# The last pair of gate columns projected behind the values, with transposes and two short attention units inside its product

## The chip, the cores and the metric

The kernel runs on one core of one Trainium2 chip. The metric is the device time of one execution in microseconds (us), taken as the median of several runs. A core has five engines that each run their own stream in order and meet only at semaphores: TensorE (PE, matrix products), VectorE (DVE), ScalarE (ACT), GpSimd (POOL) and SyncE (SP, which here issues the DMA transfers).

## What is computed

One layer of a hybrid backbone over 256 context tokens and 1024 latent tokens, all float32. What matters here is the input projection, whose columns the kernel takes in 16 pairs of 128, and the attention that follows.

```python
h = rms_norm(x, lp['norm1_g']) * (1 + sc1) + sh1
proj = h @ lp['w_in']                       # 1024 -> 4096 columns
q, k, v, xp, ga, gb = jnp.split(proj, cuts, axis=-1)
q, k = per-head RMS norm, rotary on latent tokens
k_all = concat(cached k (512), k)           # latent queries only
attn = block_attention(q, k_all, v_all)     # context queries: 256 context keys alone
merged = sigmoid(ga) * (attn @ w_branch_a) + sigmoid(gb) * (pool @ w_branch_b)
```

## The kernel before

Every float32 operand of a product is split in a high and a low part of the type float32r, and a product is three matmuls: high by high, high by low, low by high. `project(n, j)` (matmul at L324) makes 128 columns (half j of pair n) for all 1280 tokens: eight chunks k of the 1024 inputs, nine matmuls each, into one of two PSUM halves. `hooks` is a table from a chunk number to other PE work that is issued behind that chunk. The weights of a pair are loaded by SP into `w_raw`; ACT rounds them to `w_hi` (L451), POOL subtracts to `w_lo` (L539). PE waits for `w_hi`, `w_lo` and `ps_free` (the PSUM half read out) before a product.

The first block of the kernel runs the pairs in this order: 2 of pooling input, 8 of gates, 4 of queries, the keys (K0), the values (V0). In the gate loop, hooks behind chunks 4 and 7 also multiply two blocks of the modulation weights (`ada_block`, `ada_turn`), whose rows DVE copies and adds (`loop_rows`, `loop_mods`). ACT applies the sigmoid to each gate half (L474) and SP stores it in DRAM (`gates`).

The keys of head j are normed by DVE (L715), rotated by DVE and POOL (L722, L557, L725), rounded by ACT into `kT_hi` (L518) and subtracted by POOL into `kT_lo` (L560). They lie in `kraw`, whose first buffer is the tile `stage`; the first values buffer `vraw[0]` is the same tile. ACT therefore copies the values out of PSUM (L525) only once both L560 are done (`k_lo`). PE then turns each half (ten transposes, L417) in groups n = 0 to 5, and ACT (L530, even n) and DVE (L744, odd n) copy them into `vals`. Last, ACT rounds the cached keys (L532) and POOL subtracts them (L562). All this stands behind the last product. Then a barrier of all engines, at which the semaphores are cleared (L750), ends the block.

The attention block has 16 latent units (four heads, 128 queries, 1536 keys) and 4 short ones (context queries, 256 keys). For a latent unit, a `head` is nine score matmuls (L875 to L877), the maximum on DVE (L1022 to L1025), and the exponential on ACT (L946); the scores of the next head wait for it, because they write the same PSUM banks. The opening of the block is written out: for g = 0 to 4 it issues `head(units[g // 4], g % 4)`, then for the short unit g its scores (L915 to L917), and for unit g-1 the turn (L926), the copies (L970 on ACT, L1051 on DVE) and the value product (L934). Only then come the transposes (L901) and value products (L885) of unit 0 between the further heads of unit 1. POOL splits the queries first (L987, L990; short ones L1000, L1002), after clearing `stage` (L1011) for the zero fill of `y_sum` (L862).

Of the kernel before, what the change touches and what calls it, by code (L numbers as in the profile page):

```python
# [71 lines left out]
def build(nc, io, last_block=99):  # L72
    with ExitStack() as ctx:
# [76 lines left out]
        vraw = [stage, at("vraw1", [P, TOK], F32, RHL)]  # L150
        kc_raw = at("kc_raw", [P, KV, PAST], F32, RHL + 8 * KB)

        s = {}
        for n in ("eps_r x_ss rs_used consts rope wpool_in icnt_in x_sq x_scaled xT_ps xT_outa xT_outd c_in c_sig c_silu fa_mm fa_rows fa_turn fa_mods ada_mm0 ada_mm1 ada_rows0 ada_rows1 ada_turn mods_r0 mods_r1 ada_in0 ada_in1 "
                  "mods_b h_raw h_hi_r h_lo_r w_in0 w_hi0 w_hi1 w_lo0 w_lo1 mm0 mm1 ps_free0 ps_free1 pad0 xp_in xp_used "
                  "d_done gate_r0 gate_r1 gate_st0 gate_st1 py_ps py_out py_st sq_r0 sq_r1 ss_mm rt_sq rt_r rs_mm rs_out q_raw q_sin q_cos q_fin "
                  "k_fin k_hi k_lo kout v_raw vout v_ps v_out_a v_out_d cache_in cache_hi cache_lo dve_c").split():
# [4 lines left out]
        XP_PAIRS, GATE_PAIRS, Q_PAIRS = 2, 8, 4  # L162
        G0, Q0, K0, V0 = 2, 10, 14, 15
# [7 lines left out]
        ROWS_AT = AUX[0]  # L171
        FIRST = (0, 4, 1, 5, 2, 6, 3, 7)
# [8 lines left out]
        with nc.Block() as block:  # L181
            @block.sync
            def _(sp):
# [18 lines left out]
                def load_ada(n, j):  # L202
                    if isinstance(n, int):
# [10 lines left out]
                for c in range(4):  # L214
# [3 lines left out]
                    if c == 1:  # L218
                        load_w(2)

                def store_gate(i, j):
                    sp.wait_ge(s[f"gate_r{j}"], i + 1)
                    sp.dma_start(io["gates"][bass.ds(2 * i + j, 1)].rearrange("o p n -> p (o n)"), gst[j][:]).then_inc(s[f"gate_st{j}"], 16)
                with sp.Fori(0, GATE_PAIRS - 1) as i:
                    load_w(i + G0 + 1)
                    load_ada(i + 5, 0)
                    store_gate(i, 0)
                    load_ada(i + 5, 1)
# [15 lines left out]
                for j in range(2):  # L244
                    sp.wait_ge(s["q_raw"], HEADS + j + 1)
                    sp.dma_start(io["out_k"][j], kraw[j][:, 0:CTX]).then_inc(s["kout"], 16)
                for j in range(2):
                    sp.wait_ge(s["v_raw"], j + 1)
                    if j == 1:
                        sp.dma_start(kc_raw[:], io["cache_k"]).then_inc(s["cache_in"], 16)  # L250
                        sp.wait_ge(s["k_fin"], 2)
                        sp.dma_start(vals[:, TILES:KEY_TILES, :], io["cache_v"]).then_inc(s["cache_in"], 16)
                    sp.dma_start(io["out_v"][j], vraw[j][:, 0:CTX]).then_inc(s["vout"], 16)
                sp.wait_ge(s["kout"], 32)
                sp.wait_ge(s["vout"], 32)
                for j in range(2):
                    sp.wait_ge(s[f"gate_st{j}"], 16 * GATE_PAIRS)
                sp.wait_ge(s["cache_in"], 32)

            @block.tensor  # L260
            def _(pe):
# [98 lines left out]
                for n in range(1, XP_PAIRS):  # L360
                    project(n, 0)
                    project(n, 1)
                with pe.Fori(0, GATE_PAIRS) as i:
                    for j in range(2):
                        project(i + G0, j, hooks={4: lambda: ada_block(i + 4, j), 7: lambda: ada_turn(i + 4, j)})
# [40 lines left out]
                project(V0, 1)  # L406

                for j in range(2):
                    pe.wait_ge(s["v_raw"], j + 1)
                    for q, (g, w) in enumerate(GROUPS):  # L410
# [1680 lines left out]
```

## Time and profile before

| | us |
|---|---|
| median of 3 runs | 1818.58 |
| lowest and highest run | 1817.08 and 1820.91 |
| the profiled execution | 1816.4 |
| its span, first to last instruction | 1814.5 |
| PE busy (share of the span) | 1616.6 (89%) |
| DVE, ACT, POOL busy | 898.6, 593.2, 393.8 |

The profiled execution is 1.9 us longer than its span, for what lies before the first and behind the last instruction. The median of the runs is 2.2 us above the profiled one. The views used below are the page, its windows (busy time by stretch with the granted TensorE clock, where 1.00 is 2.4 GHz and 0.50 is 1.2 GHz), and the timeline, where an entry in brackets gives the idle time before an instruction and what ended it.

### The profile page before, as it was taken

The page shows a single profiled execution, that of the slowest core. Times are in us where ns is not written, and L with a number is a line of the kernel's source. Part 1 is how long each engine was busy: PE and PEld are TensorE (multiplying, and loading weights), DVE is VectorE, ACT ScalarE, POOL GpSimd, SP SyncE. Part 2 cuts the span into 40 slices and gives each one's busy share as a digit, 9 for nine tenths or more (in the row PEclk, how much of TensorE's full clock was granted, in tenths as well). Part 3 has the DMA queues.
Part 4 walks back from the last instruction along what each step waited for, and adds up shares of the span by engine and source line. Part 5 has one row for each costly group of instructions (what it writes and reads, how often), then busy time and mean ns, then how long its engine had stood idle before and what let it go on. Part 6 is the DMA issues. An engine that isn't in the chain of part 4 may idle for free. (4 is left out here: it accounts for less than half of the span.)

```text
span 1814.5 us, 22464 instructions
## 1 busy us (share of the span) xinstructions
PE 1616.6 (89%) x8410; PEld 1278.2 (70%) x8410; DVE 898.6 (50%) x1257; ACT 593.2 (33%) x764; POOL 393.8 (22%) x252
## 2 busy tenths in 40 slices
PE   4899999999999699999999899989977399999950
PEld 4688888878887466666666588878866288888840
DVE  5560000006565666676666543341147667666638
ACT  5211121232222444444444500021123055555513
POOL 1011111112223400000000121121116234445420
PEclk8999999999999899999999999999998599999985
DMA  8133434230100500000000133213032179898945
GB/s 350 67 115 135 159 132 143 109 119 23 46 23 9 200 1 0 0 1 1 0 0 0 58 139 121 85 53 124 23 114 105 65 233 295 266 290 277 281 77 218
DMA packets 38016, 202.28 MB, mean 111 GB/s; under 512 B 4304, under 2 KB 5072, under 8 KB 27728
## 3 DMA queue, kind: packets, MB, share of 16 engines
q1 hardware_dynamic: 28752, 168.07, 24.0%
q0 software_dynamic: 9216, 33.56, 8.3%
q8 instruction: 31, 0.51, 0.1%
q14 instruction: 17, 0.14, 0.0%
HBM read 154.43 MB, written 47.19 MB: 111 GB/s over the span
## 5 line engine op out<-in xcount | busy, mean ns | idle before, releaser
L324 PE MATMUL psum<-h_hi,w_hi 128*128 128x512 f32 (+1 forms) x768 | 199.3, 368 | 7.3 <-DVE h_lo L624 5.5
L324 PE MATMUL psum<-h_lo,w_hi 128*128 128x512 f32 (+1 forms) x768 | 193.6, 361 | 0.0
L324 PE MATMUL psum<-h_hi,w_lo 128*128 128x512 f32 (+1 forms) x768 | 192.5, 359 | 0.0
L885 PE MATMUL psum<-probT,vals 128*128 128x512 f32 x384 | 190.9, 593 | 0.0
L946 ACT ACTIVATE prob<-psum,nmax 128x1536 f32<-128x1536 f32 x64 | 98.6, 1541 | 209.5 <-DVE nmax L1025 209.5
L324 PEld LDWEIGHTS psum<-h_hi,w_hi 128*128 128x128 f32 x768 | 128.7, 190 | 34.7 <-issue 14.3
L539 POOL TENSOR_TENSOR w_lo<-w_raw,w_hi 128x1024 fp32r<-128x1024 f32 x32 | 77.0, 2408 | 348.2 <-ACT w_hi L451 348.2
L901 PEld LDWEIGHTS psum<-ident,prob 128*128 128x128 f32 x768 | 93.0, 141 | 78.6 <-issue 72.7
L324 PEld LDWEIGHTS psum<-h_lo,w_hi 128*128 128x128 f32 x768 | 128.8, 190 | 23.1
L324 PEld LDWEIGHTS psum<-h_hi,w_lo 128*128 128x128 f32 x768 | 128.5, 189 | 23.1
L1022 DVE TENSOR_REDUCE rmax<-psum 128x1 f32<-128x512 f32 x192 | 128.9, 688 | 31.1 <-PE psum L877 30.8
L901 PE MATMUL psum<-ident,prob 128*128 128x128 f32 x768 | 110.7, 274 | 7.9 <-PE psum L885 7.9
L875 PE MATMUL psum<-kT_hi,q_hi 128*128 128x512 f32 x192 | 96.7, 504 | 10.1 <-POOL q_lo L990 8.7
L591 DVE COPY ada_rows<-psum 128x256 f32<-128x256 f32 x24 | 10.2, 425 | 159.7 <-PE psum L279 159.4
L853 DVE COPY probT<-psum 128x512 f32<-128x512 f32 x64 | 44.3, 691 | 85.3 <-PE psum L901 85.3
L1645 POOL DMA_INDIRECT y_sum<-yst,y_row x32 | 74.9, 2340 | 26.0 <-POOL y_row L1643 26.0
L877 PE MATMUL psum<-kT_hi,q_lo 128*128 128x512 f32 x192 | 76.1, 396 | 0.0
L853 ACT COPY probT<-psum 128x512 f32<-128x512 f32 x128 | 70.0, 586 | 18.0 <-PE psum L901 18.0
L876 PE MATMUL psum<-kT_lo,q_hi 128*128 128x512 f32 x192 | 75.3, 392 | 0.0
L885 PEld LDWEIGHTS psum<-probT,vals 128*128 128x128 f32 x384 | 61.6, 190 | 17.4 <-issue 16.1
L1817 DVE TENSOR_TENSOR gu_lo<-gu_raw,gu_hi 128x3072 fp32r<-128x3072 f32 x15 | 50.4, 3358 | 47.5 <-ACT gu_hi L1760 47.5
L987 POOL CAST q_hi<-qT 128x512 fp32r (+1 forms) x16 | 9.7, 609 | 295.4 <-PE psum L877 295.4
(326 smaller groups left out, 3026.3 us busy)
## 6 DMA issues: line engine op xcount, KB each, us to landing
gu_raw<-in_w_gu SPq DMA_DIRECT2D x16, 2048.0 KB, 9.4
ada<-in_w_ada SPq DMA_DIRECT2D x20, 1024.0 KB, 4.8
w_raw<-in_w_in SPq DMA_DIRECT2D x16, 1024.0 KB, 4.8
dn_raw<-in_w_dn SPq DMA_DIRECT2D x16, 1024.0 KB, 6.9
gates<-gst SPq DMA_DIRECT2D x16, 640.0 KB, 3.0
wm_raw<-in_w_merge SPq DMA_DIRECT2D x4, 1536.0 KB, 7.8
y_sum<-stage SPq DMA_DIRECT2D x12, 512.0 KB, 11.9
xt<-in_x SPq DMA_DIRECT2D x10, 512.0 KB, 8.0
```

The costliest lines, as they stand in the source:

```text
L324: mm = pe.matmul(psum[:, par_sets[j] + g:par_sets[j] + g + w], a[j][:, k, :], b[:, k, g:g + w], start=(k == 0 and a is w_hi and b is h_hi) ...
L539: nc.gpsimd.tensor_tensor(w_lo[j][:], w_raw[:, :, j * P:(j + 1) * P], w_hi[j][:], ALU.subtract).then_inc(s[f"w_lo{j}"], 1)
L853: copy(probT[b][g % 2][:], psum[:, TP + 512 * b:TP + 512 * b + 512]).then_inc(s[f"a_t_out{b}"], 1)
L875: pe.matmul(o, q_hi[x.par][:, g, :], kT_hi[:, x.kv, k], start=True, stop=False)
L876: pe.matmul(o, q_hi[x.par][:, g, :], kT_lo[:, x.kv, k], start=False, stop=False)
L877: pe.matmul(o, q_lo[x.par][:, g, :], kT_hi[:, x.kv, k], start=False, stop=True).then_inc(s["a_scored"], 1)
L885: mm = pe.matmul(psum[:, PV + 512 * x.par:PV + 512 * x.par + 512], vals[:, x.key0 // P + c, x.kv * HD:(x.kv + 1) * HD], probT[b][g % 2][:] ...
L901: mm = pe.transpose(psum[:, o:o + P], prob[x.par][:, h, c * P:(c + 1) * P], ident[:])
L946: nc.scalar.activation(prob[x.par][:, g, 0:x.keys], psum[:, SC:SC + x.keys], ACT.Exp, bias=nmax[:, x.par, g:g + 1], scale=SCALE, accum_out ...
L1022: ins = nc.vector.reduce_max(rmax[:, b:b + 1], psum[:, SC + 512 * b:SC + 512 * (b + 1)], AX.X)
L1645: nc.gpsimd.indirect_dma_start(io["y_sum"], bass.IndirectOffsetOnAxis(y_row[j][:], 0), yst[j][:], None, compute_op=ALU.add).then_inc(s[f"e ...
L1817: tt(gu_lo[q][:, 0:GU_FIRST, :], gu_raw[q][:, 0:GU_FIRST, :], gu_hi[q][:, 0:GU_FIRST, :], ALU.subtract).then_inc(s[f"e_gu_lo{q}"], 1)
```

## The change

The pair order of the projection becomes 2 pooling, 7 gates, 4 queries, keys, values, and then the eighth gate pair (L0). Modulation blocks 4 to 11 had been the hooks of the eight gate pairs; now the second pooling pair carries the hooks of block 4, the gate loop those of blocks 5 to 11, and L0 none. The value transposes (`turn_v`) become hooks: groups 0 to 2 behind chunks 4 to 6 of the second half of the values, groups 3 to 5 behind chunks 1 to 3 of L0's first half. The cached keys are loaded earlier to another place and split between the weight splits of L0. The short units 0 and 1 run as hooks of L0 (scores, turn, values), with their own tiles and semaphores; the attention block keeps units 2 and 3, and POOL has split unit 2's queries already. The clearing of `stage` moves behind the first short value step. The late sigmoids use the tile of the cached keys and `stage`, and SP stores them before the barrier.

```diff
-        XP_PAIRS, GATE_PAIRS, Q_PAIRS = 2, 8, 4
-        G0, Q0, K0, V0 = 2, 10, 14, 15
+        XP_PAIRS, GATE_PAIRS, Q_PAIRS = 2, 7, 4
+        G0, Q0, K0, V0, L0 = 2, 9, 13, 14, 15
...
+                    for j in range(2):
+                        project(n, j, hooks={4: lambda: ada_block(4, j), 7: lambda: ada_turn(4, j)})
...
-                project(V0, 1)
...
+                def turn_v(n):
+                    j, (g, w) = n // 3, GROUPS[n % 3]
                     pe.wait_ge(s["v_raw"], j + 1)
...
+                def early_score(z):
+                    pe.wait_ge(s["s_q"], 2 * z + 2)
+                    pe.wait_ge(s["k_lo"], 2)
...
+                    for g in range(GRP):
+                        o = psum[:, AUX[0] + CTX * g:AUX[0] + CTX * (g + 1)]
+                        pe.matmul(o, sq_hi[:, g, :], kT_hi[:, 0, 0:CTX], start=True, stop=False)
+                        pe.matmul(o, sq_hi[:, g, :], kT_lo[:, 0, 0:CTX], start=False, stop=False)
+                        mm = pe.matmul(o, sq_lo[:, g, :], kT_hi[:, 0, 0:CTX], start=False, stop=True)
+                    mm.then_inc(s["s_scored"], 1)
...
+                def early_turn(z):
+                    pe.wait_ge(s["s_normed"], z + 1)
+                    for c in range(2):
+                        for h in range(GRP):
...
+                def early_value(z):
+                    pe.wait_ge(s["gate_r0"], GATE_PAIRS + 1)
+                    pe.wait_ge(s["s_pv_out"], z)
...
+                project(V0, 1, hooks={4: lambda: turn_v(0), 5: lambda: turn_v(1), 6: lambda: turn_v(2)})
+                project(L0, 0, hooks={1: lambda: turn_v(3), 2: lambda: turn_v(4), 3: lambda: turn_v(5), 5: lambda: early_score(0)})
+                project(L0, 1, hooks={0: lambda: early_turn(0), 1: lambda: early_value(0), 2: lambda: early_score(1),
+                                      5: lambda: early_turn(1), 6: lambda: early_value(1)})
...
+                v_rows(0)
+                split(L0, 0)
+                act.wait_ge(s["ck_in"], 16)
                 nc.scalar.copy(kT_hi[:, :, TOK:KEYS], kc_raw[:]).then_inc(s["cache_hi"], 1)
+                v_out(0)
+                v_out(2)
+                v_rows(1)
+                split(L0, 1)
+                v_out(4)
+                early_exp(0)
+                act.wait_ge(s["cache_lo"], 1)
+                late_gate(0)
...
+                early_turned(0)
+                early_values(0)
+                early_exp(1)
+                early_turned(1)
+                early_values(1)
+                late_gate(1)
...
+                    if c in (1, 2):
+                        loop_rows(4, c - 1)
+                        loop_mods(4, c - 1)
...
-        short = [Unit(z, z // 2, z % 2 * P, 0, CTX, 0) for z in range(4)]
...
+        short = [Unit(z, z // 2, z % 2 * P, 0, CTX, 0) for z in range(SHORT_EARLY, 4)]
...
-    order = [6, 7] + list(range(8, 16)) + [0, 1, 2, 3] + [4, 5]
+    order = [6, 7] + list(range(8, 15)) + [0, 1, 2, 3] + [4, 5] + [15]
```

PE before, the end of the second half of the values (L324, the last chunk) and the transposes (L417). A semaphore in brackets is what the instruction waits for; `vraw_113` is the second values buffer.

```order
L324 MATMUL psum<-h_hi,w_lo_86 128x512 x2
L324 MATMUL psum<-h_hi,w_lo_86 128x256
L417 MATMUL psum<-ident,stage 128x128 [waits b1_rs_out,b1_v_raw]
L417 MATMUL psum<-ident,stage 128x128 x7
L417 MATMUL psum<-ident,stage 128x128 [waits b1_v_out_a]
L417 MATMUL psum<-ident,stage 128x128
L417 MATMUL psum<-ident,vraw_113 128x128 [waits b1_v_out_d,b1_v_raw]
L417 MATMUL psum<-ident,vraw_113 128x128 x3
L417 MATMUL psum<-ident,vraw_113 128x128 [waits b1_v_out_a]
L417 MATMUL psum<-ident,vraw_113 128x128 x3
L417 MATMUL psum<-ident,vraw_113 128x128 [waits b1_v_out_d]
L417 MATMUL psum<-ident,vraw_113 128x128
```

PE after, in the middle of the same half (its product is now L338, the transposes L429): the end of chunk 4, hook, chunk 5, and the next hook.

```order
L338 MATMUL psum<-h_hi,w_lo_86 128x256
L429 MATMUL psum<-ident,stage 128x128 [waits b1_rs_out,b1_v_raw]
L429 MATMUL psum<-ident,stage 128x128 x3
L338 MATMUL psum<-h_hi,w_hi_84 128x512 x2
L338 MATMUL psum<-h_hi,w_hi_84 128x256
L338 MATMUL psum<-h_lo,w_hi_84 128x512 x2
L338 MATMUL psum<-h_lo,w_hi_84 128x256
L338 MATMUL psum<-h_hi,w_lo_86 128x512 x2
L338 MATMUL psum<-h_hi,w_lo_86 128x256
L429 MATMUL psum<-ident,stage 128x128 [waits b1_v_raw]
L429 MATMUL psum<-ident,stage 128x128 x3
```

The first transpose with its wait for `v_raw` now has three chunks of the values' product queued behind it.

ACT before, from the second rounding of keys to the end of the first block:

```order
L518 CAST kT_hi<-kraw_112 128x1280 [waits b1_k_fin]
L525 COPY stage<-psum 128x1280 [waits b1_mm0,b1_kout,b1_k_lo]
L525 COPY vraw_113<-psum 128x1280 [waits b1_mm1]
L530 COPY vals<-psum 128x4x128 [waits b1_v_ps,b1_k_fin,b1_q_fin]
L530 COPY vals<-psum 128x2x128 [waits b1_v_ps]
L530 COPY vals<-psum 128x4x128 [waits b1_v_ps]
L532 CAST kT_hi<-kc_raw 128x2x512 [waits b1_cache_in]
```

ACT after, from the early exponentials of unit 0 (L588) to the end of the block; L582 is the late sigmoid, L594 and L598 copy the turned scores and the values of a short unit:

```order
L588 ACTIVATE sprob_early,short_sum<-psum,short_nmax 128x256 x3
L582 ACT_TABLE_LOAD [waits b1_mm0]
L582 ACTIVATE gst_late_115<-psum 128x1280 [waits b1_cache_lo]
L594 COPY sprobT_early_119<-psum 128x512 [waits b1_s_turned,b1_s_pv,b1_vout,b1_v_ps]
L598 COPY qT<-psum 128x4x128 [waits b1_s_pv]
L588 ACT_TABLE_LOAD [waits b1_s_turned]
L588 ACTIVATE sprob_early,short_sum<-psum,short_nmax 128x256 [waits b1_s_neg_max]
L588 ACTIVATE sprob_early,short_sum<-psum,short_nmax 128x256 x3
L594 COPY sprobT_early_119<-psum 128x512 [waits b1_s_pv,b1_s_turned]
L598 COPY qT<-psum 128x4x128 [waits b1_s_pv]
L582 ACT_TABLE_LOAD
L582 ACTIVATE stage<-psum 128x1280 [waits b1_mm1]
```

The last work of ACT in the block is now a sigmoid of the product that ends last, where it was the rounding of the cached keys. The load of the last sigmoid's function table stands ahead of the wait for `mm1`.

DVE before, the third and fourth steps of the attention opening (L1022 maximum of a head, L1040 maximum of a short unit, L1047 its norm, L1051 its copy):

```order
L1040 TENSOR_REDUCE short_max<-psum 128x4
L1041 TENSOR_SCALAR short_nmax<-short_max 128x4
L1034 RECIPROCAL einv<-esum 128x1
L1036 TENSOR_SCALAR prob_2663<-prob_2663,einv 128x1536
L1046 RECIPROCAL short_inv<-short_sum 128x4
L1047 TENSOR_TENSOR sprob<-sprob,short_inv 128x1024
L1022 TENSOR_REDUCE rmax<-psum 128x1 x3
L1024 TENSOR_REDUCE rmax<-rmax 128x1
L1025 TENSOR_SCALAR nmax<-rmax 128x1
L1051 COPY sprobT_2679<-psum 128x512
L1040 TENSOR_REDUCE short_max<-psum 128x4
```

DVE after, from the copy of the last short unit (L1171) on:

```order
L1171 COPY sprobT_3033<-psum 128x512
L1154 RECIPROCAL einv<-esum 128x1
L1156 TENSOR_SCALAR prob_3019<-prob_3019,einv 128x1536
L1142 TENSOR_REDUCE rmax<-psum 128x1 x3
L1144 TENSOR_REDUCE rmax<-rmax 128x1
L1145 TENSOR_SCALAR nmax<-rmax 128x1
L1154 RECIPROCAL einv<-esum 128x1
L1156 TENSOR_SCALAR prob_3019<-prob_3019,einv 128x1536
L1142 TENSOR_REDUCE rmax<-psum 128x1 x3
L1144 TENSOR_REDUCE rmax<-rmax 128x1
```

Between two maxima of a head stand only the norm of the head before, where there were also a copy, a maximum and a norm of a short unit.

## Rows read from the trace of the kernel before

**Rows 1.** The page: head, and DMA issues of the gates (last: us to landing).

```profile
span 1814.5 us, 22464 instructions
...
gates<-gst SPq DMA_DIRECT2D x16, 640.0 KB, 3.0
```

**Rows 2.** Windows: length, busy us per engine (instructions), granted clock, DMA share, GB/s.

```profile
585.00:602.00 17.00, 5.25 (x22) 3.71 (x20) 1.81 (x3) 6.22 (x7) 6.74 (x6) 0.58 0.33 110
...
602.00:645.00 43.00, 30.95 (x142) 22.00 (x143) 31.71 (x53) 19.21 (x49) 17.96 (x14) 0.94 0.45 171
```

**Rows 3.** Timeline: start us, us, engine, line, operation, count, [idle before].

```profile
570.77 0.54 PEld L324 LDWEIGHTS psum<-h_hi,w_hi 128*128 128x128 f32 x3
...
570.77 4.97 DVE L722 TENSOR_TENSOR rtmp<-kraw,sin 32x1024 f32<-32x1024 f32 x4 [0.34 <-DVE kraw L715]
...
579.69 0.75 PE L324 MATMUL psum<-h_hi,w_hi 128*128 128x512 f32 x3
...
583.72 2.91 POOL L560 TENSOR_TENSOR kT_lo<-kraw,kT_hi 128x1280 fp32r<-128x1280 f32 x1 [2.52 <-ACT kT_hi L518]
...
584.38 0.74 PE L324 MATMUL psum<-h_hi,w_lo 128*128 128x512 f32 x3
...
586.66 1.23 ACT L525 COPY stage<-psum 128x1280 f32<-128x1280 f32 x1 [3.02 <-POOL kT_lo L560]
...
587.94 2.56 PE L417 MATMUL psum<-ident,stage 128*128 128x128 f32 x10 [2.81 <-ACT stage L525]
```

**Rows 4.** Timeline, from the last split of the first block to the first attention score.

```profile
595.34 2.34 POOL L562 TENSOR_TENSOR kT_lo<-kc_raw,kT_hi 128x1024 fp32r<-128x1024 f32 x1 [8.72 <-ACT kT_hi L532]
...
599.04 0.95 POOL L1011 MEMSET stage<- 128x1024 f32 x1 [1.36 <-POOLq L750]
...
602.04 0.80 PE L875 MATMUL psum<-kT_hi,q_hi 128*128 128x512 f32 x1 [8.70 <-POOL q_lo L990]
```

**Rows 5.** Timeline of PE, the beginning of the attention block.

```profile
608.52 0.50 PE L875 MATMUL psum<-kT_hi,q_hi 128*128 128x512 f32 x1 [1.41 <-ACT prob L946]
...
618.46 0.80 PE L875 MATMUL psum<-kT_hi,q_hi 128*128 128x512 f32 x1
...
625.12 1.96 PE L934 MATMUL psum<-sprobT,vals 128*128 128x512 f32 x4 [1.71 <-ACT sprobT L970]
...
641.94 3.26 PE L934 MATMUL psum<-sprobT,vals 128*128 128x512 f32 x4 [3.31 <-ACT sprobT L970]
...
646.65 0.48 PE L875 MATMUL psum<-kT_hi,q_hi 128*128 128x512 f32 x1
```

**Rows 6.** Timeline, second pooling pair: start of its product, end of the second pooled channel.

```profile
88.63 0.83 PE L324 MATMUL psum<-h_hi,w_hi 128*128 128x512 f32 x3 [0.51 <-issue]
...
100.39 1.69 DVE L694 TENSOR_TENSOR dpool<-dpool,xpad 128x256 f32<-128x256 f32 x2
```

**Rows 7.** Windows after two idle stretches of PE (columns as in rows 2).

```profile
587.90:594.20 6.30, 5.12 (x20) 3.71 (x20) 1.81 (x3) 2.65 (x4) 0.00 (x0) 0.50 0.61 208
...
602.00:604.80 2.80, 2.76 (x7) 2.20 (x8) 0.69 (x1) 0.00 (x0) 1.82 (x2) 0.50 1.03 281
```

**Rows 8.** Timeline of PE, one short unit: scores, turn, next scores, values.

```profile
605.53 0.27 PE L915 MATMUL psum<-kT_hi,sq_hi 128*128 128x256 f32 x1
...
606.84 0.28 PE L917 MATMUL psum<-kT_hi,sq_lo 128*128 128x256 f32 x1
...
612.66 1.10 PE L926 MATMUL psum<-ident,sprob 128*128 128x128 f32 x8 [1.77 <-DVE sprob L1047]
...
613.51 0.36 PE L915 MATMUL psum<-kT_hi,sq_hi 128*128 128x256 f32 x1
...
617.06 1.95 PE L934 MATMUL psum<-sprobT,vals 128*128 128x512 f32 x4 [1.89 <-ACT sprobT L970]
```

**Rows 9.** Timeline of ACT, first sigmoid of the gate loop.

```profile
132.42 1.28 ACT L474 ACT_TABLE_LOAD   x1 [13.06 <-PE psum L324]
...
133.71 1.24 ACT L474 ACTIVATE gst<-psum 128x1280 f32<-128x1280 f32 x1
```

More of the change, by code:

```diff
@@ L149, in build @@
         kraw = [stage, at("kraw1", [P, TOK], F32, RKV + 40 * KB)]
-        vraw = [stage, at("vraw1", [P, TOK], F32, RHL)]
-        kc_raw = at("kc_raw", [P, KV, PAST], F32, RHL + 8 * KB)
+        vraw = [stage, at("vraw1", [P, TOK], F32, RKV + 45 * KB)]
+        kc_raw = at("kc_raw", [P, KV, PAST], F32, RKV + 50 * KB)
+        gst_late = [at("gst_late0", [P, TOK], F32, RKV + 50 * KB), stage]
+        sq_hi = at("sq_hi", [P, GRP, P], F32R, RW)
+        sq_lo = at("sq_lo", [P, GRP, P], F32R, RW + 2 * KB)
+        sprob_early = at("sprob_early", [P, GRP, CTX], F32, RW + 4 * KB)
+        sprobT_early = [at(f"sprobT_early{c}", [P, GRP * P], F32, RKV + (45 + 2 * c) * KB) for c in range(2)]
         s = {}
@@ L360, in _ @@
                 for n in range(1, XP_PAIRS):
[L361 to L362 removed]
+                    for j in range(2):
+                        project(n, j, hooks={4: lambda: ada_block(4, j), 7: lambda: ada_turn(4, j)})
                 with pe.Fori(0, GATE_PAIRS) as i:
                     for j in range(2):
[L365 removed]
+                        project(i + G0, j, hooks={4: lambda: ada_block(i + 5, j), 7: lambda: ada_turn(i + 5, j)})
                 pe.wait_ge(s["wpool_in"], 16)
@@ L528, in _, with v_out, late_gate @@
-                for n in range(0, 6, 2):
+                    act.wait_ge(s["v_raw"], j + 1)
+                    act.sem_inc(s[f"ps_free{j}"], 1)
+                def v_out(n):
                     act.wait_ge(s["v_ps"], n + 1)
                     nc.scalar.copy(*v_chunk(n)).then_inc(s["v_out_a"], 1)
-                act.wait_ge(s["cache_in"], 32)
-                nc.scalar.copy(kT_hi[:, :, TOK:KEYS], kc_raw[:]).then_inc(s["cache_hi"], 1)
+                def late_gate(j):
+                    act.wait_ge(s[f"mm{j}"], L0 + 1)
+                    nc.scalar.activation(gst_late[j][:], psum[:, par_sets[j]:par_sets[j] + TOK], ACT.Sigmoid).then_inc(s[f"gate_r{j}"], 1)
@@ new lines, in early_exp, with early_turned @@
+                def early_exp(z):
+                    act.wait_ge(s["s_neg_max"], z + 1)
+                    act.wait_ge(s["s_turned"], 2 * z)
+                    for g in range(GRP):
+                        nc.scalar.activation(sprob_early[:, g, :], psum[:, AUX[0] + CTX * g:AUX[0] + CTX * (g + 1)], ACT.Exp,
+                                             bias=short_nmax[:, g:g + 1], scale=SCALE, accum_out=short_sum[:, g:g + 1]).then_inc(s["s_exped"], 1)
+                def early_turned(z):
+                    act.wait_ge(s["s_turned"], 2 * z + 1)
+                    act.wait_ge(s["s_pv"], z)
+                    nc.scalar.copy(sprobT_early[0][:], psum[:, AUX[0]:AUX[0] + 512]).then_inc(s["s_out_a"], 1)
```

130 lines of the change are left out of this document (89 added, 41 removed).

## The prediction

> **What bounds the kernel now.** I read the page first, then the windows around the end of the first block, then the timeline there. PE is busy for 89% of the span, and in the projection its chunks stand back to back. So work that only changes its place inside the projection is neither won nor lost, and time can only come from the stretches where PE idles. The windows show two [rows 2]. From 585 to 602, PE is busy for 5.25 of 17 us, at a mean granted clock of 0.58. From 602 to 645, the opening of the attention, it is busy for 30.95 of 43 us. The profiled execution has a span of 1814.5 us [rows 1] and a time of 1816.4; the median of the runs is 1818.6, 2.2 above it. I work out a difference and add it to the median.
>
> The timeline explains the first stretch. The last product begins at 570.77, and its last matmul ends at 584.38 + 0.74 = 585.12 [rows 3]. The values leave PSUM only from 586.66, when POOL has subtracted the second keys (583.72 + 2.91 = 586.63). The transposes start at 587.94. Behind them come the cached keys, whose subtraction ends at 597.68; the barrier lets POOL go on at 599.04, and the first attention scores start at 602.04 [rows 4]. In the opening, PE waits for the chain of scores, maximum and exponential of one head at a time, with short units in between, and the last value product of a short unit waits until 641.94 [rows 5].
>
> **Part one, the order of the pairs.** One gate pair without its modulation hooks moves behind the values, and two modulation blocks move into the second pooling pair. All of it is full PE work in either place: nothing. I looked for a new wait at the front. The second pooling pair begins at 88.63 [rows 6]; a chunk takes (579.69 - 570.77) / 5 = 1.78 us [rows 3], so the hook behind chunk 7 comes at about 88.6 + 8 x 1.78 + 1 = 104. It needs DVE's copy of the modulation rows, which now stands behind the second pooled channel, done at 100.39 + 1.69 = 102.1 [rows 6]; with a copy of about half a us it comes in time. The margin is a little over 1 us; if it fails, the cost is under 1 us.
>
> **Part two, the value transposes as hooks: a new wait.** The first hook stands behind chunk 4 of the second half of the values. The product starts where it did (relative to the keys nothing changed), so PE reaches it at 579.69 on the old time line. The transposes read `vraw[0]`, which is the tile of the first keys, and ACT fills it only behind both key subtractions. That chain is unchanged: DVE's rotation begins at 570.77, POOL's subtraction ends at 586.63, ACT copies from 586.66, and PE could start to turn at 587.94 [rows 3]. Behind the waiting transposes three chunks are queued that had run meanwhile. The wait costs 587.94 - 579.69 = **8.3 us**. Before, the same wait was only 2.8 us, because the whole product was ahead of it.
>
> **The clock behind the wait.** After its idle stretches, PE ran at half clock: for the whole 2.8 us from 602.00, and for the 6.3 us from 587.90 in which it was partly idle [rows 7]. Half of such a time is lost: 1.4 to 3.2 us. PE is fully busy afterwards, as at 602, but the record of 587.90 follows the same place; I take the middle, **2.2 us**.
>
> **The work in the hooks.** Eight transposes of a short unit cost 613.51 - 612.66 = 0.85 us at full clock, its twelve score matmuls 606.84 - 605.53 + 0.12 = 1.43 us, its value product about 1.4 us (a row of two matmuls from 617.06, the next scores from 618.46) [rows 5, 8]. The 20 value transposes cost 20 x 0.106 = 2.1 us, and changing between kinds of work some 0.4: **2.5 us**. Two short units cost 2 x (0.85 + 1.43 + 1.4) = **7.4 us**. A turn stands three chunks (5.3 us) behind its scores. Before, the time from the end of the scores (606.84 + 0.28 = 607.12) to the turn (612.66) was 5.5 us [rows 8]; with the changes of kind I take **0.9 us** for both units. The Exp table can be loaded ahead of the wait for the maximum, so it isn't in that chain. The rest has cover: the weight splits of the late pair, the cached keys and the sigmoid of its first half all lie beside full chunks. Sum: 8.3 + 2.2 + 2.5 + 7.4 + 0.9 = 21.3 us. Taking away the moved pair, the products end at 585.1 + 21.3 = 606.4 on the old time line.
>
> **The way to the attention.** Behind the last matmul come the sigmoid, 1.24 us, with some 0.15 us of its table load still to go (a load takes 133.71 - 132.42 = 1.29 us [rows 9], and only the last chunk lies beside it and the copy ahead of it), the store of 640 KB, 3.0 us in the median [rows 1], and the barrier, 599.04 - 597.68 = 1.36 us. POOL then splits at once, without clearing `stage` (0.95 us, of which 0.9 were in the way): 602.04 - 599.04 - 0.9 = 2.1 us [rows 4]. With the steps between engines that is **8.0 us**, where it was 602.04 - 585.12 = 16.9. The first attention scores come at 614.4 instead of 602.04: **12.4 us later**. The store may take up to 1.5 us longer, since it competes with nothing but was never alone either.
>
> The trace shows a table load of 1.29 us from its start to that of the sigmoid, with nothing between. The Trainium skill, page "ScalarE: Activation LUTs", section "What ACT_TABLE_LOAD costs", puts a switch of function sets at about 2.66 us, for it adds a drain to the load. By that price the last sigmoid would start some 1.4 us later and the sum would be 1.4 higher; by the row it isn't. I go by the row.
>
> **The opening of the attention.** Up to the value product at 625.12 the two openings are the same: two short units in both. Before, two more followed, and the second heads of unit 1 started at 646.65, 44.6 us after the first scores [rows 5]. After, three heads follow the value product (one of unit 0, the first and the second of unit 1), and nothing stands between them but their own chain. The first such chain took 608.52 - 602.04 = 6.5 us, 1.4 of them due to the half clock: 5.1 us. At full clock the second head of unit 1 would start at 625.12 + 1.4 + 2 x 5.1 = 636.7, and 9.9 us are won. But PE is idle by about 3 us before the value product and again in each chain; after such a gap the value product from 641.94 took 3.26 us. With the half clock once or twice, it is 638 to 640, and 6.6 to 8.6 are won. I take **7.8 us**, nearer to the slow end because the gaps of 3.3 us are those that brought the clock down at 641.94.
>
> **Sum.** 12.4 - 7.8 = 4.6 us slower: 1818.6 + 4.6 = **1823.2 us**.
>
> **The rivals.** (a) The same mechanism, but the clock comes back early and the opening keeps it: 1.4 instead of 2.2, 9.9 instead of 7.8. That gives 4.6 - 0.8 - 2.1 = 1.7, so 1820.3. For it speaks that the value product from 617.06, after an idle time of 1.89 us, took 1.95 us [rows 8]; against it the 3.26 us from 641.94, after 3.31 us [rows 5]. (b) The values are there in time: if the copy of the first half came before the hook is reached at 579.69, the wait of 8.3 and its clock, 2.2, fall away: 4.6 - 10.5 = -5.9, so 1812.7. It decides at 579.69, and the key subtraction ends 7 us later, so I see no way but a faster key chain than the trace has. (c) More waits: each short chain inside the product is stretched, because DVE, ACT and POOL also do the late pair's work there, by some 1.5 us each, and the half clock follows twice: 4.6 + 3 + 1.5 = 9.1, so 1827.7. The rows show one unit's chain with other work around it, which speaks against much more than the 0.9 taken. (d) A table switch costs a drain beside its load, as one could suspect where the exponential, the late sigmoid and the exponential again follow each other on ACT: with 1.4 more at the end and 0.3 at the first short value product, 1823.2 + 1.7 = 1824.9. The sigmoid of rows 9 speaks against it. That the page named above states it gives it a small chance.
>
> **How the numbers follow.** Chances: forecast 0.45, (a) 0.27, (b) 0.10, (c) 0.13, (d) 0.05. A measurement of this kernel can tell about 0.2%, 3.6 us, from no change. Faster by more: (b), with a little for what I don't see, 0.11. Within 0.2%: (a) and part of the forecast's spread below 1822.2, 0.31. Slower: 0.58. The forecast's own spread is the clock (1 us each way), the opening (1.2 down, 2.1 up), the store (1.5 up). The range goes from 1817.5, which covers (a) with the spread of the median, to 1828.5, which covers (c); (b) stays outside.
>
> **What would show it.** In the trace after, the first value transposes should carry an idle time of about 8.3 us, ended by ACT's copy of the values, and the granted clock should be 0.50 for 3 to 6 us behind it. The turns of the early units should wait for DVE by under 1 us. From the last product matmul to the first attention scores should be some 8 us, ended by SP's wait for the store. From those scores to the second head of unit 1 some 37 us. If the first transposes hardly wait, I am wrong on the side of (b); if the opening takes 35 us or less, it is (a).

## Result: slower by 0.4 to 0.55 percent, and the profile after

| kernel | median, us | lowest to highest | ratio to before, 95% interval |
|---|---|---|---|
| before | 1818.22 | 1817.08 to 1820.91 | |
| changed | 1828.26 | 1828.2 to 1829.82 | 1.0055 [1.0038, 1.0073] |
| changed, run again beside the experiments | 1827.36 | 1825.03 to 1828.74 | 1.0042 [1.0025, 1.0059] |

The loss is 10.0 us in the first comparison and 7.0 in the second, where 4.6 were forecast. The profiled execution has a span of 1826.4 us against 1814.5 [rows 1]. I split both at four points: the start of the second pooling pair's product [rows 6], the first attention scores [rows 4], the second head of unit 1 [rows 5], and the first load of the merge block that follows the attention (`pool_raw`).

| stretch, us | before | before, 2nd trace | changed | changed, 2nd trace |
|---|---|---|---|---|
| up to the second pooling pair | 88.6 | 89.1 | 87.2 | 87.1 |
| to the first attention scores | 513.4 | 513.4 | 525.9 | 525.7 |
| opening of the attention | 44.6 | 44.6 | 45.4 | 45.3 |
| rest of the attention | 382.3 | 382.2 | 382.2 | 382.3 |
| the rest | 785.6 | 787.9 | 785.7 | 782.7 |

In these two kernels the three middle rows repeat within 0.2 us from trace to trace, so a single trace can carry them. The first row goes from 86.7 to 89.1 us over the fourteen traces of this case, the last from 782.2 to 788.2. The forecast was +12.4 in the second row and -7.8 in the third; measured are +12.5 and +0.7.

The second row, in the timeline of PE and ACT after (start, us, engine, line, operation, idle time before and what ended it), as in [rows 3]:

```profile
557.07 1.23 ACT L572 COPY stage<-psum 128x1280 f32<-128x1280 f32 x1 [2.99 <-POOL kT_lo L647]
...
558.35 1.12 PE L429 MATMUL psum<-ident,stage 128*128 128x128 f32 x4 [8.01 <-ACT stage L572]
559.12 1.42 PE L338 MATMUL psum<-h_hi,w_hi 128*128 128x512 f32 x3
560.34 1.27 PE L338 MATMUL psum<-h_lo,w_hi 128*128 128x512 f32 x3
561.40 0.99 PE L338 MATMUL psum<-h_hi,w_lo 128*128 128x512 f32 x3
...
585.17 1.09 PE L453 MATMUL psum<-ident,sprob_early 128*128 128x128 f32 x8 [0.31 <-DVE sprob_early L859]
...
598.49 1.09 PE L453 MATMUL psum<-ident,sprob_early 128*128 128x128 f32 x8 [0.30 <-DVE sprob_early L859]
...
604.06 0.76 PE L338 MATMUL psum<-h_hi,w_lo 128*128 128x512 f32 x3
...
613.10 0.79 PE L992 MATMUL psum<-kT_hi,q_hi 128*128 128x512 f32 x1 [8.28 <-POOL q_lo L1107]
```

The first value transposes wait 8.01 us for ACT's copy, which waits for POOL's second key subtraction. The chunk behind them runs at half clock: three steps of 0.59 us pitch at full clock take 1.22, 1.06 and 0.83, and the transposes ahead of them 0.77 instead of 0.35, together 1.8 us lost. The two early turns wait 0.3 us each. From the end of the last product, 604.82, to the first scores are 8.28 us.

The third row is where the forecast went wrong. PE, DVE and POOL in the second step of the opening:

```profile
619.84 0.50 PE L992 MATMUL psum<-kT_hi,q_hi 128*128 128x512 f32 x1 [1.39 <-ACT prob L1063]
...
628.00 1.97 PE L1043 MATMUL psum<-ident,sprob 128*128 128x128 f32 x8 [5.82 <-DVE sprob L1167]
...
641.89 3.75 PE L1051 MATMUL psum<-sprobT,vals 128*128 128x512 f32 x4 [3.31 <-ACT sprobT L1087]
...
651.46 0.77 PE L992 MATMUL psum<-kT_hi,q_hi 128*128 128x512 f32 x1 [2.92 <-ACT prob L1063]
...
658.46 0.50 PE L992 MATMUL psum<-kT_hi,q_hi 128*128 128x512 f32 x1 [0.54 <-ACT prob L1063]
```

```profile
619.74 1.65 DVE L1161 TENSOR_SCALAR short_nmax<-short_max 128x4 f32<-128x4 f32 x1
...
621.45 2.14 DVE L1156 TENSOR_SCALAR prob<-prob,einv 128x1536 f32<-128x1536 f32 x1
...
623.71 4.23 DVE L1167 TENSOR_TENSOR sprob<-sprob,short_inv 128x1024 f32<-128x1024 f32 x1
627.87 1.87 DVE L1142 TENSOR_REDUCE rmax<-psum 128x1 f32<-128x512 f32 x3
```

```profile
620.41 0.96 POOL L1131 MEMSET stage<- 128x1024 f32 x1
621.32 1.47 POOL L1127 CAST wm_hi<-wm_raw 128x1536 fp32r<-128x1536 f32 x1
622.86 4.00 POOL L1129 TENSOR_TENSOR wm_lo<-wm_raw,wm_hi 128x1536 fp32r<-128x1536 f32 x1
626.82 1.60 POOL L1104 CAST q_hi<-qT 128x512 fp32r<-128x512 f32 x1
```

POOL splits the merge weights behind the value step of the *last* short unit. There were four short units and there are two, so this work now stands in the second step. The normalising multiplication L1167 takes 4.23 us: POOL's subtraction ends at 622.86 + 4.00 = 626.86, and DVE 1.08 us later. PE waits 5.82 us. In the kernel before, the same subtraction stood in the fourth step, where DVE was at maxima over PSUM (628.95 and 631.72), and the next multiplication of two SBUF tiles came only at 636.12 and took 1.36 us:

```profile
630.43 3.45 POOL L1010 TENSOR_TENSOR wm_lo<-wm_raw,wm_hi 128x1536 fp32r<-128x1536 f32 x1
```

What the clock does in the opening (windows: length, busy us per engine, granted clock, DMA share, GB/s), first of before, in its first trace, then of after:

```profile
602.04:646.65 44.61, 32.60 (x153) 23.65 (x154) 31.86 (x54) 20.38 (x51) 17.92 (x14) 0.93 0.43 163
```

```profile
613.10:658.46 45.36, 30.93 (x105) 22.71 (x105) 28.85 (x45) 14.10 (x31) 12.88 (x9) 0.74 0.42 167
...
628.00:633.00 5.00, 5.00 (x21) 4.74 (x22) 3.08 (x7) 2.11 (x3) 1.68 (x2) 0.50 1.02 401
...
641.89:658.46 16.57, 13.11 (x34) 8.91 (x34) 7.30 (x15) 3.90 (x6) 1.88 (x2) 0.63 0.00 0
```

PE has 105 instructions where it had 153, and is busy almost as long. A mean clock of 0.74 is 2 x 0.26 x 45.4 = 23.6 us at the half level; before it was 2 x 0.07 x 44.6 = 6.2. The last window runs from the second value product of a short unit to the end of the opening. That product comes 641.89 - 613.10 = 28.8 us behind the first scores, where before it came after 625.12 - 602.04 = 23.1.

### The profile page after: what moved, and what is told of

The parts are those of the page before. It is cut to its first block and busy times, and to the rows that moved or that the text cites. A ratio compares the mean times of both kernels' runs of the same rounds, so it can differ in the third digit from the quotient of the medians.

```text
span 1826.4 us, 22442 instructions
## 1 busy us (share of the span) xinstructions
PE 1622.2 (89%) x8410; PEld 1282.6 (70%) x8410; DVE 902.9 (49%) x1257; ACT 597.2 (33%) x767; POOL 395.5 (22%) x252
## 5 line engine op out<-in xcount | busy, mean ns | idle before, releaser
L338 PE MATMUL psum<-h_hi,w_hi 128*128 128x512 f32 (+1 forms) x768 | 201.1, 370 | 7.4 <-DVE h_lo L726 5.5
L338 PE MATMUL psum<-h_lo,w_hi 128*128 128x512 f32 (+1 forms) x768 | 193.3, 360 | 0.0
L338 PE MATMUL psum<-h_hi,w_lo 128*128 128x512 f32 (+1 forms) x768 | 192.5, 359 | 0.0
L338 PEld LDWEIGHTS psum<-h_hi,w_hi 128*128 128x128 f32 x768 | 129.1, 191 | 35.2 <-issue 15.3
L1142 DVE TENSOR_REDUCE rmax<-psum 128x1 f32<-128x512 f32 x192 | 129.4, 689 | 42.5 <-PE psum L994 42.4
L338 PEld LDWEIGHTS psum<-h_lo,w_hi 128*128 128x128 f32 x768 | 128.6, 190 | 23.2
L338 PEld LDWEIGHTS psum<-h_hi,w_lo 128*128 128x128 f32 x768 | 128.3, 189 | 23.1
L1937 DVE TENSOR_TENSOR gu_lo<-gu_raw,gu_hi 128x3072 fp32r<-128x3072 f32 x15 | 50.4, 3358 | 47.7 <-ACT gu_hi L1880 47.7
```

What stands on the lines that cost most here:

```text
L338: mm = pe.matmul(psum[:, par_sets[j] + g:par_sets[j] + g + w], a[j][:, k, :], b[:, k, g:g + w], start=(k == 0 and a is w_hi and b is h_hi) ...
L1142: ins = nc.vector.reduce_max(rmax[:, b:b + 1], psum[:, SC + 512 * b:SC + 512 * (b + 1)], AX.X)
L1937: tt(gu_lo[q][:, 0:GU_FIRST, :], gu_raw[q][:, 0:GU_FIRST, :], gu_hi[q][:, 0:GU_FIRST, :], ALU.subtract).then_inc(s[f"e_gu_lo{q}"], 1)
```

## The experiments

My theory: the change loses time at two places, the late value copy (8.0 us of waiting and the clock behind it), and POOL's moved work in the opening, which holds DVE up and brings PE's clock down. The rival for the second: with half the short units gone, the chain of scores, maximum and exponential has no cover, and the opening would be as long wherever POOL works. In the diffs `m_`, `a_` and `s_` semaphores are those of the listing. All three sets of runs stood beside runs of before: 1820.06 us (e1 to e4), 1820.37 (again, e5 to e7), 1820.55 (before again, e8 to e10).

| kernel | median, us | ratio to before, 95% interval | to first scores | opening | mean clock in it |
|---|---|---|---|---|---|
| before | | | 513.4 | 44.6 | 0.93 |
| changed | 1827.36 | 1.0042 [1.0025, 1.0059] | 525.9 | 45.4 | 0.74 |
| e1 | 1820.49 | 1.0003 [0.9993, 1.0013] | 526.1 | 38.1 | 0.86 |
| e2 | 1819.17 | 0.9994 [0.9985, 1.0004] | 521.5 | 42.7 | 0.82 |
| e3 | 1810.88 | 0.9938 [0.9921, 0.9956] | 516.0 | 40.3 | 0.80 |
| e4 | 1823.35 | 1.0017 [1.0007, 1.0027] | 513.3 | 48.4 | 0.90 |
| e5 | 1811.13 | 0.9954 [0.9937, 0.997] | 506.9 | 47.7 | 0.84 |
| e6 | 1816.88 | 0.9979 [0.997, 0.9989] | 516.0 | 43.2 | 0.81 |
| e7 | 1815.87 | 0.9977 [0.9967, 0.9988] | 511.5 | 42.5 | 0.96 |
| e8 | 1827.59 | 1.0034 [1.0019, 1.0049] | 525.7 | 40.4 | 0.92 |
| e9 | 1807.32 | 0.9928 [0.9912, 0.9945] | 516.1 | 35.9 | 0.90 |
| e10 | 1807.09 | 0.993 [0.9912, 0.9948] | 507.0 | 43.2 | 0.94 |

**e1, POOL paced.** The changed kernel with POOL's work of the opening put off.

```diff
+                        one = isinstance(x.u, int) and x.u == 1
+                        if one:
+                            pool.wait_ge(s["a_scored"], 9)
                         split(x)
+                        if one:
+                            pool.wait_ge(s["a_scored"], 12)
+                            nc.gpsimd.memset(stage[:, 0:D], 0.0).then_inc(s["a_zero"], 1)
+                            pool.wait_ge(s["a_scored"], 18)
+                            pool.wait_ge(s["m_wm_in"], 16)
+                            nc.gpsimd.tensor_copy(wm_hi[0][:], wm_raw[:, :, 0:P]).then_inc(s["m_wm_hi0"], 1)
...
-                    if z == len(short) - 1:
...
-                    if z == 0:
-                        nc.gpsimd.memset(stage[:, 0:D], 0.0).then_inc(s["a_zero"], 1)
```

> The changed kernel, with POOL's work in the attention opening put off: the query split of unit 1 waits for the scores of the third head, the clearing of stage for the fourth head, the rounding and subtraction of the first merge weights for the second head of unit 1. Nothing else is moved. Theory (POOL's two-input and rounding work, moved into the middle of the opening, blocks DVE, whose norm of a short unit took 4.2 us there instead of 1.2): that norm is back at 1.2 to 1.4 us, the wait of 5.8 us before the first turn falls to 1 or 2 us, and from the first attention scores to the second head of unit 1 it takes 36 to 39 us instead of 45.4; time 1819 to 1822. Rival (the opening is as long because of the half clock and each head's own chain): 43 to 46 us, time 1826 to 1829.

The multiplication and the turn behind it:

```profile
623.88 1.23 DVE L1172 TENSOR_TENSOR sprob<-sprob,short_inv 128x1024 f32<-128x1024 f32 x1
...
625.16 1.09 PE L1043 MATMUL psum<-ident,sprob 128*128 128x128 f32 x8 [1.81 <-DVE sprob L1172]
```

The multiplication is back at 1.23 us, the wait goes from 5.82 to 1.81, and the opening falls from 45.4 to 38.1 us, near the 36.8 that I had forecast. The second value product comes 23.1 us behind the first scores (614.12 to 637.19), as before. The time is that of before. The hook's wait stays at 8.01 us.

**e4, the same work moved early in the kernel before.** The reverse test: `if z == len(short) - 1:` becomes `if z == 1:` there, nothing else.

> The kernel before, with one change: POOL rounds and subtracts the first merge weights behind the second short unit's step instead of the fourth's. Theory (POOL blocks DVE when these 6 us of work fall into the second and third steps of the opening): a DVE instruction that works on two tiles of SBUF takes 3 to 5 us there, the opening grows from 44.6 us by 2 to 5 us, time 1820 to 1823. Rival (their place does nothing): 44 to 45 us, time 1817 to 1820.

```profile
617.30 4.06 POOL L1010 TENSOR_TENSOR wm_lo<-wm_raw,wm_hi 128x1536 fp32r<-128x1536 f32 x1
...
618.15 4.28 DVE L1047 TENSOR_TENSOR sprob<-sprob,short_inv 128x1024 f32<-128x1024 f32 x1
```

In the kernel before, with all four short units, the same pair of instructions meets, DVE's takes 4.28 us, the opening grows by 3.8 us (its second value product comes 26.2 us behind the first scores instead of 23.1) and the median by 3.3, just over the 1823 that I had expected as the most. So the meeting costs time with all the units there as well.

**e8, PE kept busy in that wait.** The changed kernel with POOL left alone, and twelve products of no use ahead of PE's wait for the first turn.

```diff
+                    if z == 0:
+                        for _ in range(12):
+                            pe.matmul(psum[:, TC[0]:TC[0] + 512], kT_hi[:, 0, 0:P], kT_hi[:, 0, 0:512], start=True, stop=True)
                     pe.wait_ge(s["c_normed"], z + 1)
```

> The changed kernel, GpSimd's work where the change put it, with twelve 128x512 products of no use, about 0.43 us each at full clock, on PE in the 5.8 us in which it waits for VectorE before the first short turn. No wait gets shorter. Theory (part of the loss is TensorE's clock, which is at 0.50 in the 5 us behind this wait and at 1.00 in e1): the turn takes 1.0 us instead of 2.0, the clock stays at 1.00 in the 5 us behind it, opening 42 to 43.5 us instead of 45.3, total 2 to 3 us under the changed kernel's 1827.5. Rival (the chain over VectorE sets the opening, not PE's pace): clock up, but opening 45 us and total 1827 all the same.

```profile
621.26 2.88 PE L1042 MATMUL psum<-kT_hi 128*128 128x512 f32 x12
627.28 1.09 PE L1046 MATMUL psum<-ident,sprob 128*128 128x128 f32 x8 [3.13 <-DVE sprob L1170]
```

```profile
622.95 4.27 DVE L1170 TENSOR_TENSOR sprob<-sprob,short_inv 128x1024 f32<-128x1024 f32 x1
```

```profile
612.39:652.81 40.42, 27.05 (x117) 20.08 (x118) 28.92 (x45) 14.09 (x31) 12.94 (x9) 0.92 0.47 188
```

DVE is held up as before (4.27 us), and the turn can start no earlier (8.2 us behind the scores that precede it, 619.08 to 627.28, as 619.84 to 628.00). But with the clock kept the turn takes 1.09 us instead of 1.97, and the opening is 40.4 us: 4.9 less than in the changed kernel, of which the wait itself gave nothing. Only about half a us of it is won up to the second value product (28.3 us behind the first scores, at 640.73); behind it the rest of the opening takes 12.1 us instead of 16.6, at a mean clock of 1.00. Not all of that need be the work of the twelve products: e2, below, has the same opening without any of them and takes 13.8 us there. I had priced the products at 0.43 us; they took 0.24 each at full clock, so half of the wait was left empty, and the clock held all the same. The time is a different matter: the ten times fall in two groups, four from 1820.1 to 1821.8 and six from 1827.0 to 1830.2, and the trace is of the lowest. It shows the turn and the work behind it at full clock; the median, 1827.59, shows no gain over the changed kernel. What happened in the other six no trace tells.

**e2, the values copied early.** In the changed kernel ACT copies the first half of the values out behind the first key subtraction, ahead of the second rounding of keys.

```diff
-                for j in range(2):
-                    act.wait_ge(s["k_fin"], j + 1)
-                    nc.scalar.copy(kT_hi[:, j, 0:TOK], kraw[j][:]).then_inc(s["k_hi"], 1)
-                act.wait_ge(s["k_lo"], 2)
...
+                nc.scalar.copy(kT_hi[:, 0, 0:TOK], kraw[0][:]).then_inc(s["k_hi"], 1)
+                act.wait_ge(s["k_lo"], 1)
...
                 v_rows(0)
+                act.wait_ge(s["k_fin"], 2)
+                nc.scalar.copy(kT_hi[:, 1, 0:TOK], kraw[1][:]).then_inc(s["k_hi"], 1)
+                act.wait_ge(s["k_lo"], 2)
                 split(L0, 0)
```

> The changed kernel, with one change on ACT: the first half of the values is copied out of PSUM as soon as POOL has subtracted the first keys, which is all that reads the tile stage, instead of both; the second rounding of keys comes behind it. Theory (the wait of 8.0 us at the first value transposes is the way of the keys through the shared tile): the wait falls to 2.5 to 3 us, and the half clock behind it may fall away; time 1821 to 1824. Rival (something else is late next, such as the weight split of the late pair on ACT and POOL, which still stands behind both key subtractions): the 5 us come back as a wait before the late pair's product, time 1827 to 1829.

```profile
554.45 0.66 PE L429 MATMUL psum<-ident,stage 128*128 128x128 f32 x4 [2.62 <-ACT stage L566]
...
561.45 0.41 PE L429 MATMUL psum<-ident,stage 128*128 128x128 f32 x2 [2.42 <-ACT vals L572]
```

The wait falls to 2.62 us, but ACT's copy of the transposed values now stands behind the second key subtraction, and the third hook waits 2.42 us for it. Of 8.0 us of waiting 3.0 are gone, and with the clock 4.4 us on the way to the scores. Rival (b) of the prediction had put this at 10.5.

The median is 8.2 us below that of the changed kernel, lower than the 1821 to 1824 that I expected. Part of it lies in the opening, which this edit doesn't touch and which takes 42.7 us instead of 45.4. Up to the second value product it is the same, 28.9 us; behind it the clock is at 0.88 instead of 0.63:

```profile
639.04:652.84 13.80, 9.36 (x34) 5.97 (x35) 7.16 (x15) 3.90 (x6) 1.87 (x2) 0.88 0.00 0
```

So with the same instructions in the opening, these last steps take 13.8 or 16.6 us according to where the clock falls. What decides that no run here shows.

**e3, both mends and later hooks.** e1 and e2 together; the second key rounding doesn't hold the late pair's split, the hooks `turn_v` stand two chunks later, and the values come first.

```diff
-                project(V0, 1, hooks={4: lambda: turn_v(0), 5: lambda: turn_v(1), 6: lambda: turn_v(2)})
-                project(L0, 0, hooks={1: lambda: turn_v(3), 2: lambda: turn_v(4), 3: lambda: turn_v(5), 5: lambda: early_score(0)})
+                project(V0, 1, hooks={6: lambda: turn_v(0), 7: lambda: turn_v(1)})
+                project(L0, 0, hooks={0: lambda: turn_v(2), 2: lambda: turn_v(3), 3: lambda: turn_v(4), 4: lambda: turn_v(5), 5: lambda: early_score(0)})
```

> The changed kernel with POOL paced as in e1, the values copied early as in e2, the late pair's first weight split put before the second key subtraction on ACT and POOL, and the value transposes two chunks later. Theory: no wait of over 1 us is left inside the products (8.0 and about 2 us of half clock gone), and the opening takes 36 to 39 us: against the changed kernel 16 to 20 us less, time 1808 to 1813, faster than the kernel before by 5 to 10 us. Rival (the work of the short units costs as much inside the products as in the opening): 1816 to 1820.

No value transpose waits any more; the first scores come 9.9 us sooner than in the changed kernel, which is the wait of 8.0 and the 1.8 of the clock. The opening, 40.3 us, is longer than the 36 to 39 that I expected. The total is 0.62% [0.44, 0.79] below before.

**e6, e3 with POOL as in the change.**

> As e3, with GpSimd's memset, weight split and query split where the change put them. Theory (GpSimd's operands in SBUF hold VectorE up in the second step of the opening): the normalising copy takes 4.2 us instead of 1.2, the turn behind it waits 6 us, opening 45 to 48 us instead of 40.3, total 1810.9 + 5 to 8 = 1816 to 1819. Rival (the early value copies alone make e3 fast, GpSimd's place is worth little): 1811 to 1813.

The opening is 43.2 us against 40.3 and the median 6.0 us above that of e3. Its turn waits 6.60 us for DVE. The trace's difference, 2.9 us, is below the 5 to 8 that I expected; the median's is inside. The 2.9 are two parts: up to the second value product e6 is 4.2 us longer (29.5 against 25.2), and behind it 1.3 shorter (13.8 against 15.1). Another 3.4 us of the traces' difference lie behind the attention (786.7 against 783.3).

**e5, no early short units.** e3 with all four short units in the opening (`SHORT_EARLY = 0`, and the hooks `early_score`, `early_turn` and `early_value` gone).

> As e3, with all four short units back in the opening of the attention. The two early units cost the stage of products about 3.6 us each plus 0.6 us of waits (7.8 us together). Theory (the units bring less than they cost, since the order of the opening has waits of its own): first scores some 8 us earlier than in e3 (595 us on its trace), opening 44 to 45 us instead of 40.3, total 1807 (1804 to 1810). Rival (short units early are what makes e3 fast): opening 50 us or more, as PE then waits 8 us more on ScalarE and GpSimd in it, total 1813 or more. Gain of the early units in e3 = this time less that of e3.

The first scores come 9.1 us sooner and the opening is 7.4 longer; the median, 1811.13, is that of e3 within the intervals. Neither theory had it: the early units neither pay nor cost. The 47.7 us are longer than before's 44.6, and the clock in it is lower, 0.84 against 0.93; e10, below, with the clock at 0.94, takes 43.2.

**e7, the kernel before with the two mends.** Its first half of the values is copied behind the first key subtraction; POOL's memset and weight split wait for `a_scored` 12 and 18.

> The kernel before, with the first half of the values copied out behind the first key subtraction and with GpSimd's memset and weight split moved behind the scores of unit 1. Theory (e3's gain belongs to the projected pair behind the values with all its hooks): the seam between the product and the first scores, 16.9 us before, loses at most the 2.8 us in which PE waits for the value copy; opening 42 to 45 us; total 1817 (1814.5 to 1819.5). Rival (the mends alone do it): 1811 or less, as e3.

1.9 us are won on the way to the scores and 2.1 in the opening, and 4.5 by the medians: between the two theories, nearer to the first. By the medians e5 and e3 are 4.7 and 5.0 us faster than e7. But its eight times fall in two groups, four from 1811.5 to 1814.0 and four from 1817.7 to 1818.1, and its median lies between them. And the two stretches don't show it: together they take 554.0 us in e7, 554.6 in e5 and 556.3 in e3. So it is not shown that the late gate pair gains anything where its hooks stand, even with both collisions gone. What the traces have instead is a shorter end of the kernel, behind all that the change touches (see "The total").

**e9 and e10, PE kept busy in e3 and e5.** Five useless products ahead of the first scores, five (four) ahead of the first turn, seven (four) ahead of the second value product, in the form of e8.

> As e3, with such products in three waits of PE: five before the first scores, five before the first short turn, seven before the second short values (3.3 us wait). Theory: half-clock stretches behind these three points get shorter or go, opening 36 to 38.5 us instead of 40.3, total 1808 (1806 to 1810). Rival (pace of PE is covered by the chain of VectorE and ScalarE): 1811, opening 40.

> As e5 (all four short units in the opening), with five products before the first scores, four before the first short turn and four before the second short values. Theory: opening 43 to 45 us instead of 47.7, total 1807 (1805 to 1809.5). Rival: 1811, opening 47 to 48.

The opening of e3, then that of e9:

```profile
603.27:643.59 40.32, 28.38 (x106) 21.14 (x106) 24.03 (x45) 14.09 (x31) 4.72 (x5) 0.80 0.27 108
```

```profile
605.07:640.99 35.92, 27.12 (x118) 20.32 (x118) 23.81 (x45) 14.11 (x31) 4.74 (x5) 0.90 0.29 118
```

With 12 instructions more, PE is busy for 1.3 us less, and the opening is 4.4 us shorter; that of e10 is 4.5 shorter than e5's. The medians fall by 3.6 and 4.0 us, of four runs each; the intervals of the ratios overlap with those of e3 and e5. Both are 0.7% faster than before, and again equal to each other.

**Both kernels again.** The kernel before:

> The kernel before itself, for a second trace. Theory: the first attention scores start 513.4 us behind the second pooling pair and the opening takes 44.6 us, as in the first trace; what differs between its runs lies in the first 90 us and behind the attention. Rival: the opening itself scatters by more than 2 us, and single traces can't carry the comparison of the openings.

It took 1820.29 us, with an opening of 44.6 us as in its first trace. The changed kernel:

> The changed kernel itself, beside the variants. Both theories: 10 us (8 to 12) slower than the kernel before; first attention scores to second head of unit 1 in 45.4 us; wait for the value copies at the first value transposes 8.0 us.

It was 7.0 us slower than before, under the 8 to 12 expected, with an opening of 45.3 us and a wait of 8.01 us.

## Where the prediction held and where it failed

**Part one, the order of the pairs.** Forecast nothing. The stretch up to the first scores grew by 12.5 us. The waits, the clock and the way to the attention, as measured below, with the 2.5 forecast for the transposes and the 9.1 that e5 shows for the two units, make 8.0 + 1.8 + 2.5 + 9.1 + 8.3 - 16.9 = 12.8. Nothing is left for the order.

**The wait at the first value transposes.** Forecast 8.3, measured 8.01; e3 removed it. **The clock behind it:** forecast 2.2 of 1.4 to 3.2, measured 1.8. **The way to the attention:** forecast 8.0, measured 8.28. The first scores came 12.5 us later where 12.4 had been forecast. The sigmoid stood where rows 9 put it: ACT's table load began at 603.71 and the sigmoid at 605.01, 1.30 us later, with no drain between. Rival (d) is out, and with it, for this kernel, the 2.66 us that the Trainium skill states on the page "ScalarE: Activation LUTs", section "What ACT_TABLE_LOAD costs".

**The two early units.** Forecast 7.4 us of work and 0.9 of waiting. The two turns waited 0.61 us, and without the units (e5) the first scores came 9.1 us sooner, so the work was about a us more than I had priced. Rival (c), which stretched these chains inside the product, is wrong in its place: nothing was stretched there. Its half clock came in the opening instead.

**The opening: the term that failed.** Forecast -7.8, measured +0.7. The step says that up to the value product at 625.12 "the two openings are the same: two short units in both". They weren't. The step before it had noted that POOL no longer clears `stage` on the way to the attention, and took 0.9 us for it, but did not ask what POOL now meets at the new place; and the weight split moved though no line of it changed, since its condition names the last short unit. Both now stand in the second step, beside DVE's operations on SBUF. That is one part of the 8.5 us by which the step was wrong: the value product that it starts from came 28.8 us behind the first scores instead of 23.1, 5.7 us late. e1, with POOL's work out of the way, has it at 23.1 again, and e4, which brings the meeting into the kernel before, at 26.2.

The other 2.9 us lie behind that product, where the step had 36.8 - 23.1 = 13.7 us for three heads with their half clock, and the changed kernel took 16.6. e2 and e6, with POOL's work as in the change, took 13.8 at a mean clock of 0.88. At 0.63 the half level took 2 x 0.37 x 16.6 = 12.3 us, at 0.88 it took 2 x 0.12 x 13.8 = 3.3. So the 13.7 held where the half level was short, and for this kernel the half clock was priced too low. e1 took 15.0 us there, which is the 1.3 between its opening of 38.1 and my 36.8. Why the clock falls for so long in one kernel and not in the other stays open.

**The total.** The forecast of 1823.2 with a range up to 1828.5 stood nearer to the measured time than its own terms deserved; that is luck. By the two stretches, the change costs 12.5 + 0.7 = 13.2 us; the medians say 10.0 and 7.0. The rest lies in what the change doesn't touch. Behind the last matmul, the four traces of before's order (before twice, e4, e7) take 65.5 to 66.8 us, the ten of the changed order 62.8 to 63.8: 2.7 us less in the mean, and no overlap. DVE's steps there take the same time in all. The loads `y<-y_sum` don't: their median time to landing is 9.5 to 11.1 us in before's order and 8.3 to 9.2 in the changed one. The code of these loads is the same in both, and why they differ isn't known. With this, 13.2 - 2.7 = 10.5 us is near the first comparison. It also belongs to the 9.2 us that e3 is faster than before: its two stretches give 1.7 of them, this end 2.7, and the rest stays open.

## What to carry to other kernels

When a change takes items out of a list, look for work whose place is tied to the last item: it moves without a line of the diff, and it must be priced where it lands, against what the neighbouring engines do there. A hook that reads something PE doesn't make itself belongs behind the point where the other engine is done with it, not where PE's own order first allows it. And a wait of PE costs more than its length where the work behind it runs at half clock: with useless products in three waits, the openings of e9 and e10 took 4.4 and 4.5 us less than those of e3 and e5, and the medians 3.6 and 4.0. Last, a gain of a few us in the median isn't yet a gain of the stretch that was changed: fix points in both traces and compare stretch by stretch.

## What the runs showed of the hardware

In these traces work of POOL on SBUF doesn't slow DVE down a little: it stops it. DVE's multiplication of two SBUF tiles, 128x1024, took 1.23 us alone (e1) and 4.23, 4.27 and 4.28 us beside POOL's subtraction, and ended 1.08 us behind it (changed kernel); POOL's subtraction took 4.00 us instead of 3.47 in e1, and its cast at 626.82, which had to wait for DVE in turn, 1.60 instead of 0.61. DVE's maxima over PSUM beside POOL's next subtraction (627.87, 1.87 us for three) were not held. The Trainium skill, page "SBUF — State Buffer", section "SBUF: two separate sides", says that DVE, with two inputs in SBUF, and a GpSimd operation that reads SBUF share a pair of ports as an exclusive lock. The trace agrees in these numbers. Operations of DVE with one input tile were held too: `prob` times `einv` at 621.45 took 2.14 us beside POOL's cast, where the next one, at 634.09, took 1.02, and the small one at 619.74 took 1.65 us instead of 0.17 and ended at 621.39, with POOL's memset (621.37).

TensorE's granted clock was 0.50, 1.2 GHz, behind PE's waits of 8.28, 5.82, 3.31 and 2.92 us in the changed kernel's opening, and stayed at 1.00 behind the second of them where 2.88 us of it were filled (e8). In the changed kernel the half level took 23.6 of 45.4 us; in e7, the opening with a mean clock of 0.96, it took 2 x 0.04 x 42.5 = 3.4.
